# Blocks of the normalised activations 512 instead of 544 columns apart, and their tile 256 bytes further on

## What is computed

```
first block:  h = [16 meta tokens, x];  a = rmsnorm(h)
              h += concat(pool(a), attention(a), stick_breaking(a)) @ w_out      # mixer, 272 tokens
              a = rmsnorm(h);  h += (silu(a @ w_gate) * (a @ w_up)) @ w_down     # FFN 0
second block: FFN 1 (swiglu, 1024 -> 2816 -> 1024, norms before and after)
              mixer: a @ w_mix_in, convolution and chunkwise mLSTM, @ w_mix_out
              FFN 2 (as FFN 1)
```

## Time and profile before

| | us |
|---|---|
| median of 3 runs | 844.18 |
| the three runs | 840.53, 844.18, 844.36 |
| profiled execution | 842.73 |
| its span, first to last instruction | 840.9 |
| PE busy | 815.0 |
| DVE busy | 538.0 |
| ACT busy | 427.5 |

### The profile page before, as it was taken

One profiled execution on the slowest core, in us unless ns is written; L12 is line 12 of the kernel. 1 busy time (PEld: TensorE's weight loads), 2 busy tenths in 40 slices (PEclk: granted clock), 3 DMA queues, 4 the chain that ended last, 5 costly groups with the idle time before them and its releaser, 6 DMA issues.

```text
span 840.9 us, 12339 instructions
## 1 busy us (share of the span) xinstructions
PE 815.0 (97%) x4807; PEld 715.3 (85%) x4807; DVE 538.0 (64%) x633; ACT 427.5 (51%) x553; POOL 19.7 (2%) x24
## 2 busy tenths in 40 slices
PE   6999997999999999999999999999999999999997
PEld 6989886888888888988888888899887988888886
DVE  5664523676665666786656665876778776666665
ACT  5356542754444445854444446635445754454444
POOL 0000000000000000000000000000440000000000
PEclk8999987999999999999999999999999999999999
DMA  6632122265555455465554554432335555555431
GB/s 259 253 121 101 57 95 100 98 226 183 194 200 193 176 183 196 141 237 196 200 185 176 189 198 163 163 151 101 114 137 201 178 218 184 194 200 193 175 131 50
DMA packets 20653, 141.07 MB, mean 168 GB/s; under 512 B 2432, under 2 KB 2688, under 8 KB 4112
## 3 DMA queue, kind: packets, MB, share of 16 engines
q1 hardware_dynamic: 20048, 138.56, 45.3%
q0 software_dynamic: 576, 2.10, 0.7%
HBM read 139.60 MB, written 1.05 MB: 167 GB/s over the span
## 4 chain that ended last, share of the span: by engine, by line
PE 85%; DVE 7%; ACT 4%; issue 2%; POOL 1%; DMA 1%; DVEq 0%; SPq 0%; ACTq 0%
PE ps L1325 84%; DVE wlo L911 2%; ACT whi L608 1%; PE ps L1331 1%; DMA ident<-ident_in 1%; DVE arena L1292 0%; DVE x L1090 0%; ACT squared L623 0%; DVE xa L922 0%; DVE sb_parts L1074 0%; PE ps L1526 0%; DVE arena L1072 0%; POOL arena L591 0%; DVE arena L1302 0%; ACT arena L879 0%
## 5 line engine op out<-in xcount | busy, mean ns | idle before, releaser
L1325 PE MATMUL ps<-xa,whi 128*128 128x512 f32 (+2 forms) x1808 | 505.0, 348 | 0.8 <-DVE ytmp L1262 0.8
L1325 PE MATMUL ps<-xa,wlo 128*128 128x256 f32 (+1 forms) x1408 | 395.3, 283 | 0.0
L911 DVE TENSOR_TENSOR wlo<-raw,whi 128x2048 fp32r<-128x2048 f32 x128 | 294.1, 2298 | 103.1 <-ACT whi L608 103.0
L1325 PEld LDWEIGHTS ps<-xa,whi 128*128 128x128 f32 x1808 | 315.8, 190 | 45.5 <-issue 3.0
L1325 PEld LDWEIGHTS ps<-xa,wlo 128*128 128x128 f32 x1408 | 267.0, 190 | 1.1
L608 ACT ACTIVATE whi<-raw 128x2048 fp32r<-128x2048 f32 x128 | 244.2, 1908 | 12.1 <-PE ps L1325 11.9
L1325 PE MATMUL ps<-whi,hhi 128*128 128x512 f32 x240 | 93.8, 391 | 0.0
L1325 PE MATMUL ps<-whi,hlo 128*128 128x512 f32 x240 | 93.7, 390 | 0.0
L1325 PE MATMUL ps<-wlo,hhi 128*128 128x512 f32 x240 | 93.5, 390 | 0.0
L794 ACT ACTIVATE hhi<-arena 128x512 fp32r<-128x512 f32 x30 | 19.0, 633 | 89.0 <-PE ps L1325 82.5
L780 ACT ACTIVATE arena<-ps 128x512 f32<-128x512 f32 x33 | 19.7, 596 | 87.5 <-PE ps L1325 87.3
(11 more groups left out here) (190 smaller groups left out, 531.3 us busy)
## 6 DMA issues: line engine op xcount, KB each, us to landing
raw<-wstream SPq DMA_DIRECT2D x129, 1024.0 KB, 4.8
gain_row<-rows_in POOLq DMA_DIRECT2D x4, 512.0 KB, 4.2
x<-x_in SPq DMA_DIRECT2D x2, 512.0 KB, 4.0
out<-x SPq DMA_DIRECT2D x4, 256.0 KB, 2.1
xg<-const_in SPq DMA_DIRECT2D x1, 840.0 KB, 9.4
small<-small_in SPq DMA_DIRECT2D x1, 152.0 KB, 5.8
ident<-ident_in SPq DMA_DIRECT2D x1, 64.0 KB, 4.4
arena<-meta_in SPq DMA_DIRECT2D x1, 64.0 KB, 4.4
```

Source lines behind the costliest of these rows:

```text
L911: nc.vector.tensor_tensor(wlo[slot][:], raw[slot][:], whi[slot][:].bitcast(F32), ALU.subtract).then_inc(lo_ready, 1)
L1325: return nc.tensor.matmul(o, lhsT, rhs, start=start, stop=stop, skip_group_check=True)
```

## The change

From the first FFN on xa is used through a second view, `xn`, of the same memory, with blocks of 512 columns one behind the other. The first block's products keep the old view. Two tiles of 64 columns (256 bytes) that nobody uses are allotted, one before and one after xa, so xa starts 256 bytes later and all that follows it 512 bytes later. Instructions, shapes and waits are the same.

```diff
+        sb("before_xa", [P, 64])
         xa = sb("xa", [P, KT, 2 * TOK], F32R)
+        sb("after_xa", [P, 64])
         ya = sb("ya", [P, KT, 2 * SEQ], F32R)
...
+        xn = xa[:].rearrange("p a b -> p (a b)")[:, 0:KT * 2 * SEQ].rearrange("p (a b) -> p a b", a=KT)
...
-                    nc.scalar.activation(xa[:, kt, 0:SEQ], turn_place(k, kt), ACT.Copy, scale=vec(gain, kt)).then_inc(xa_hi_ready, 1)
+                    nc.scalar.activation(xn[:, kt, 0:SEQ], turn_place(k, kt), ACT.Copy, scale=vec(gain, kt)).then_inc(xa_hi_ready, 1)
...
-                        xa[:, kt, SEQ:2 * SEQ], turn_place(k, kt), vec(gain, kt),
-                        xa[:, kt, 0:SEQ].bitcast(F32), ALU.mult, ALU.subtract).then_inc(xa_ready, 1)
+                        xn[:, kt, SEQ:2 * SEQ], turn_place(k, kt), vec(gain, kt),
+                        xn[:, kt, 0:SEQ].bitcast(F32), ALU.mult, ALU.subtract).then_inc(xa_ready, 1)
...
-                    mm(ps[:, bank, :], whi[slot][:, w], xa[:, kt, 0:2 * SEQ], kt == 0, False)
-                    ins = mm(ps[:, bank, 0:SEQ], wlo[slot][:, w], xa[:, kt, 0:SEQ], False, kt == KT - 1)
+                    mm(ps[:, bank, :], whi[slot][:, w], xn[:, kt, 0:2 * SEQ], kt == 0, False)
+                    ins = mm(ps[:, bank, 0:SEQ], wlo[slot][:, w], xn[:, kt, 0:SEQ], False, kt == KT - 1)
```

More of the change, by code:

```diff
@@ L1355, in columns_tile @@
                     w = slice(kt * 256 + a * P, kt * 256 + (a + 1) * P)
-                    mm(o, whi[slot][:, w], xa[:, kt, skip:n], kt == 0, False)
-                    mm(o, whi[slot][:, w], xa[:, kt, n + skip:2 * n], False, False)
-                    ins = mm(o, wlo[slot][:, w], xa[:, kt, skip:n], False, kt == KT - 1)
+                    mm(o, whi[slot][:, w], (xa if n == TOK else xn)[:, kt, skip:n], kt == 0, False)
+                    mm(o, whi[slot][:, w], (xa if n == TOK else xn)[:, kt, n + skip:2 * n], False, False)
+                    ins = mm(o, wlo[slot][:, w], (xa if n == TOK else xn)[:, kt, skip:n], False, kt == KT - 1)
                 return ins
@@ L1377, in first_paired_unit @@
                         w = slice(kt * 256 + a * P, kt * 256 + (a + 1) * P)
-                        mm(ps[:, bank + a, 0:SEQ], whi[slot][:, w], xa[:, kt, 0:SEQ], kt == 0, False)
-                        mm(ps[:, bank + a, 0:SEQ], wlo[slot][:, w], xa[:, kt, 0:SEQ], False, False)
+                        mm(ps[:, bank + a, 0:SEQ], whi[slot][:, w], xn[:, kt, 0:SEQ], kt == 0, False)
+                        mm(ps[:, bank + a, 0:SEQ], wlo[slot][:, w], xn[:, kt, 0:SEQ], False, False)
                 for kt in range(KT):
@@ L1383, in first_paired_unit @@
                         w = slice(kt * 256 + a * P, kt * 256 + (a + 1) * P)
-                        ins = mm(ps[:, bank + a, SEQ:2 * SEQ], whi[slot][:, w], xa[:, kt, SEQ:2 * SEQ], False, kt == KT - 1)
+                        ins = mm(ps[:, bank + a, SEQ:2 * SEQ], whi[slot][:, w], xn[:, kt, SEQ:2 * SEQ], False, kt == KT - 1)
                 return ins
@@ L1398, in first_columns_unit @@
                         w = slice(kt * 256 + c, kt * 256 + c + P)
-                        mm(o, whi[slot][:, w], xa[:, kt, 0:SEQ], kt == 0 and c == 0, False)
-                        mm(o, wlo[slot][:, w], xa[:, kt, 0:SEQ], False, False)
+                        mm(o, whi[slot][:, w], xn[:, kt, 0:SEQ], kt == 0 and c == 0, False)
+                        mm(o, wlo[slot][:, w], xn[:, kt, 0:SEQ], False, False)
                 for kt in range(KT):
@@ L1404, in first_columns_unit @@
                         w = slice(kt * 256 + c, kt * 256 + c + P)
-                        ins = mm(o, whi[slot][:, w], xa[:, kt, SEQ:2 * SEQ], False, kt == KT - 1)
+                        ins = mm(o, whi[slot][:, w], xn[:, kt, SEQ:2 * SEQ], False, kt == KT - 1)
                 return ins
@@ L1437, in small_product @@
                     w = slice(col + kt * width, col + (kt + 1) * width)
-                    mm(o, small_hi[:, w], xa[:, kt, 0:n], kt == 0, False)
-                    mm(o, small_hi[:, w], xa[:, kt, n:2 * n], False, False)
-                    ins = mm(o, small_lo[:, w], xa[:, kt, 0:n], False, kt == KT - 1)
+                    mm(o, small_hi[:, w], (xa if n == TOK else xn)[:, kt, 0:n], kt == 0, False)
+                    mm(o, small_hi[:, w], (xa if n == TOK else xn)[:, kt, n:2 * n], False, False)
+                    ins = mm(o, small_lo[:, w], (xa if n == TOK else xn)[:, kt, 0:n], False, kt == KT - 1)
                 return ins
```

## The result

The changed kernel took 848.97 us (median of 6 runs, 847.31 to 849.82) against 844.18 before (840.53 to 844.65); the ratio is 1.0063, with a 95% interval of 1.0042 to 1.0085. The forecast was 834.3, the sign wrong and the time outside the range. Of the cases it was rival 3, with 850, to which I had given 0.09.

A forecast was written before the change was run, and what follows sets the result against it. PE's matmul pace was taken as the bound; savings of 6.9 (loop turns), 0.3 and 0.2 (opening units) and 1.9 us (mixer) summed to 9.3, giving 833.4 from the profiled execution, 834.9 from the median; forecast 834.3, range 831.5 to 844.5.

The forecast's parts named there:

- rival 3: Matmuls on xa: equal starts lock the stream in a costly phase, pair 0.354 us, time 850 us; chance 0.09.
- The bound: In the FFNs PE is never idle, so time saved between matmul starts comes straight off; no new bound.
- ACT, DVE, ya and hhi at 0: Writes of xa at another address, and the moved stationary operands of down and out products, cost 0.
- The first block at 0: First block, xa still read with blocks 2176 bytes apart: change 0, bounds ±0.5 us.
- The failed step: Gate and up tiles: with equal starts a pair of 512 and 256 columns takes 0.340 us, like the down product's pace.
- The pair at 405.26: First gate pair behind the down product, 0.34 us: taken as evidence that pairs with equal starts keep the tight pace.
- every step of an extra 128 bytes throws it out again: Blocks of xa 2176 bytes apart: each step breaks PE's tight rhythm, which takes some seven matmuls to reach.
- the upper bound of the pair, 0.354: Gate and up tiles: a pair with equal starts costs at most 0.354 us, from rows showing at most 0.35.
- The 30 turns: Ten loop turns in each of three FFNs save 0.23 us a turn, 6.9 us.
- The mixer: Mixer projections, 576 matmuls of 256 columns: saves 1.9 us, bounds 0 and 2.75.
- Rival 1: Paired tiles: the address does nothing, the 256-column matmul breaks the rhythm; pair 0.348 us, time 843.5 us; chance 0.16.
- The rule of the Trainium skill: Warm matmuls take N / 2.4 GHz plus about 2.5 ns whatever the address; set aside because the trace showed 227 ns.

The follow-up runs named there:

- e2: The kernel before with only the two unused tiles added, blocks still 544 columns apart: ratio 0.9997 against before, pair 348.4 ns.
- e6: The changed kernel with the wlo matmul of the paired tiles made 512 columns wide too, which is different work: pair 453.3 ns, turn 19.95 us.
- e9: The changed kernel with only the whi pieces of the paired tiles cut to 64 stationary columns, incomplete work: pair 340.1 ns, turn 16.37 us.
- e1: The changed kernel without the two unused tiles, so blocks 512 columns apart and xa at its old start: ratio 1.0077 against before, pair 352.7 ns.
- e12: The kernel before, blocks 544 columns apart, with each paired tile's eight long matmuls ahead of its eight short ones: ratio 0.9972, turn 16.53 us.
- e4: The changed kernel with both whi and wlo pieces of the paired tiles cut to 64 stationary columns, incomplete work: pair 340.0 ns, turn 16.35 us.
- e3: The changed kernel with the first unused tile put ahead of raw, whi and wlo, moving weights and xa alike by 256 bytes: ratio 1.0077 against before.
- e10: The changed kernel with only the wlo pieces of the paired tiles cut to 64 stationary columns, incomplete work: pair 346.3 ns, turn 16.56 us.

## Why the prediction was wrong

- **The bound** held: the FFNs' time moved with PE's pace, and no wait was added there.
- **Part by part**: ACT, DVE, ya and hhi at 0 held (e2, 842.73 us). The first block at 0 held in pace: its projections' steps of 272 columns at full clock are 125.3 ns before and 125.4 after.
- **The failed step** is "I take 0.340, since the one stream with equal starts that the trace has, the down product, ends at the tight pace every time, and the pair that meets it in that state keeps it". The down product has loads of 128 columns beside matmuls of 512; the paired tile has one beside a matmul of 256. e6 and e9 show that this difference decides: with the short matmul made 512 wide equal starts give 0.227 a matmul, with the whi piece cut to 64 columns 0.340 a pair, and with neither the lock is a cycle of 0.353. Whether it is the load or the full output of the long matmul that turns it is open (see e9), and so is why. The pair at 405.26 kept the pace for one pair only, and keeps it for one pair in the changed kernel as well; I took a carry-over for a state. That equal starts are what changes the pace was right (e1, e2); which way they change it was wrong. The prediction's "every step of an extra 128 bytes throws it out again" holds only in part: in e12 an odd block costs 8 ns, but the long matmul behind it is back at 226 ns, without the seven matmuls of settling.
- **The sizes**: the upper bound of the pair, 0.354, held for the mean (353.3), though by luck: it was read off blocks 544 apart, and single pairs of the new cycle take 0.361. A pair of 0.340 exists (e4). The 30 turns gave +5.3 us in place of -6.9. The mixer gave +0.25 in place of -1.9: its short matmuls locked at 120, in the mean 119.9 against 118.7, that is 576 x 1.2 ns = 0.7 us, some of it presumably hidden by waits.
- **Rival 3** had the mechanism, a lock at a costly pace, the deciding point (a pair above 0.348) and nearly the price, 850. Its reason, the place 256 bytes past the line, was wrong: e1 at 0 and e3 at 0 against the weights are as slow. **Rival 1** had a half-truth: it blamed the short matmul, but as what leaves the address without effect, while it is what turns equal starts into a loss. What I had against it, one tight pair, was the same carry-over. Its other evidence, the mixer's tiles that never settle, I should have weighed more: the stream of short matmuls with loads of 128 columns never settled at a tight pace, and it doesn't in the changed kernel either (119.9).
- **The rule of the Trainium skill** ("TensorE: Matmul & The Clock Gate", section "Wait — 56ns, not 53.3ns?") has neither address nor load width in it. Its form fails here: a pair of the same two matmuls took 340 to 353 ns, with nothing changed but the starts and the stationary columns. The same page of the Trainium skill, section "Step-by-step: what each phase is for", says that loading the next tile's weights doesn't steal SBUF read bandwidth from the running matmul. These runs don't show whose bandwidth it is, but cutting whi to 64 stationary columns made a running stream faster (e9 against the changed kernel, 340.1 against 353.0). If that is the load's doing and not that of the narrower output, the load is not free in time.

## What to carry to other kernels

A pace that a stream of matmuls keeps in one place of a kernel holds for its whole pattern: widths, stationary columns and addresses together. Before it is carried to another place, the patterns must be the same, and one instruction at that pace behind a good stretch isn't evidence. Where 4-byte operands and short matmuls keep PE full, subtract starts over a whole period, try the order of long and short matmuls (here 0.3%, and only with the blocks 544 apart) before the addresses, and compare turns of a loop rather than single times.

## What the runs showed of the hardware

- With fp32r operands a steady stream of 512 columns starts every 226.7 ns at the granted clock of 1.00 (e6), where 512 columns at 2.4 GHz are 213.3. The step of a matmul of 256 columns in a settled tight pair is 113.3 ns in e9 and 112.5 in e4. At half clock nothing comes on top.
- Matmul timing falls into repeating cycles: tight, one of three pairs (241 + 120, 236 + 113, 233 + 117 ns), or all short ones at 120.0. The gate products with 16 stationary columns ran at 113.3 in the changed kernel and at 120.0 in e3, e6, e9 and e10, with the operands at the same addresses: more than one cycle is stable. That the state on entry picks it is my reading; no run sets that state by itself.
- What unites these cycles, perhaps reads of weights and of the moving operand that meet in SBUF, was not measured by itself and stays open.
